# A hybrid recurrent, attention and mixture-of-experts block on one core: the expert weights in a ring of 23 buffers of 1 MB instead of 11 of 2 MB

## The chip, the cores and the metric

The kernel runs on one core of one Trainium2 chip. Time is the device time of one execution in microseconds (us), the median of several runs. Lower is better.

## The reference

One layer works on 256 frames of 1024 numbers, all in float32. A mixer comes first: an input projection, a gated linear recurrence, a forgetting attention with 16 heads, and three output projections. Then every expert's feed-forward net is applied to the frames that chose it (4 of 32 experts for each frame), and a last RMS norm closes the layer:

```python
logits = (t @ w_router) + b_router
top_v, top_i = lax.top_k(logits, TOP_K)
combine = sum(one_hot(top_i, 32) * softmax(top_v)[..., None], axis=1)
for e in range(32):
    gu = t @ w_gate_up[e] + b_gate_up[e]          # 1024 x 2048 weights
    gate = jnp.minimum(gu[:, :1024], 7.0)
    up = jnp.clip(gu[:, 1024:], -7.0, 7.0)
    glu = gate * sigmoid(1.702 * gate)
    y = ((up + 1.0) * glu) @ w_down[e] + b_down[e]  # 1024 x 1024 weights
    out = out + combine[:, e:e + 1] * y
return rmsnorm(x + out, g_final)
```

The weights of one expert are 12 MB (a MB in this text is 2^20 bytes where buffers are counted), those of all 32 are 384 MB. Every one is read once. The mixer's weights are 40 MB.

## The kernel before, in words

The program is written engine by engine, with semaphores by hand. Each of the five queues runs its instructions in the order of the code.

**The mixer** has 40 weight chunks of 1 MB (`MIX_CHUNKS`), loaded by SyncE (SP) into a ring of eight buffers (`mix`), each split into a high and a low part by ScalarE (`split`) and VectorE (`split_lower`), and used by TensorE in `chunk`. The chunks are ten groups of four; `C_WO` = 36 is the last, the output projection. After it come the router and the choice of the experts.

**The experts** are worked through in order, n = 0 to 31, in pairs p. An expert's weights are 12 chunks of 1 MB (8 of `w_gate_up`, 4 of `w_down`), loaded as six pieces of 2 MB (`load_piece`, lines 286 and 287) into a ring of 11 slots (`N_SLOTS`). The slots lie in memory that the mixer has used: `free_after` (lines 297 to 303) names for each slot the semaphore that tells when the mixer is done with it. From piece 11 on, a piece waits until TensorE has used up the piece that had its slot (`chunk_done`). Piece 0 is issued ahead of mixer chunk 36, the others after mixer chunk 39. Only the last piece of all is cut in two DMAs (lines 290 and 291).

Up to 64 frames are gathered for each expert (`gather_half`), so TensorE's matmuls have 64 rows, and two of them run side by side. For one expert TensorE runs `gate_up` (L1254, 8 chunks), waits for VectorE and ScalarE to make the activation (`glu_of`, `sigmoid_of`), transposes it (`transpose_act`, L1266), runs `down` (L1278, 4 chunks), and after ScalarE's copy `Y_copy` (L610) adds the result to four accumulators in PSUM (`scatter`, L1285). In this way the work of one expert's activation lies between its `gate_up` and its `down`; the scatter of the expert before fills part of that time.

**The end**: after the last scatter ScalarE squares and sums the accumulators, four of 512 columns (L649), VectorE adds the halves (L1027), ScalarE takes the root (L654), VectorE scales by it and by `g_final` (L1032), and SP stores two tiles of 128 frames (L344).

**GpSimd** issues three groups of DMAs: the recurrence's gate weights (L390), the experts' biases (L396, L399), and `g_final` (L411), the last when slot 6 is free for good.

## Time and profile before

| | |
|---|---|
| median of 3 runs | 1217.91 us (1216.41 to 1218.07) |
| profiled execution, own time | 1219.77 us |
| its span, first to last instruction | 1217.7 us |
| mean granted TensorE clock | 0.995 |
| TensorE matmul busy | 1164.5 us (96%) |
| DMA moved | 449.84 MB, of these 447.80 MB read from HBM |
| longest chain, by engine | PE 61%, DMA 35% |

The span is 2.07 us shorter than the profiled execution's own time, and that execution is 1.86 us longer than the median of the others. In the profile PE is TensorE's matmul and PEld its weight load. L1254 is a line of the kernel. A row's last bracket is the idle time ahead of it and what ended that. A DMA "packet" is one contiguous run that one of the core's 16 DMA engines moves. GB/s and MB in the profile are decimal.

### The profile page before, as it was taken

How to read it: one execution, taken by the hardware profiler on the slowest of the kernel's cores; microseconds unless marked ns; L12 is line 12 of the kernel's file. 1: busy time of each engine (PE TensorE's matmuls, PEld its weight loads, DVE VectorE, ACT ScalarE, POOL GpSimd, SP SyncE). 2: the span in 40 equal slices, each digit the busy share in tenths (PEclk: the TensorE clock that was granted, in tenths of full speed). 3: DMA queues.
4: the chain of work that ended last, by engine and by line, in shares of the span. 5: the costliest groups of instructions: out<-in, count | busy, mean ns of one | idle time of the engine just before them, and what ended most of it. 6: DMA issues, size and time to landing. Idle time of an engine off the chain costs nothing.

```text
span 1217.7 us, 14789 instructions
## 1 busy us (share of the span) xinstructions
PE 1164.5 (96%) x6482; PEld 609.6 (50%) x6482; DVE 339.5 (28%) x651; ACT 260.1 (21%) x432; POOL 22.7 (2%) x40
## 2 busy tenths in 40 slices
PE   8999999999999999999999999999999999999985
PEld 8998999998334333333343333333333333333321
DVE  5686976564111110101021110101010101010101
ACT  6557566444001000000011010000000000000002
POOL 3000000201000000000000000000000000000000
PEclk9999999999999999999999999999999999999998
DMA  9954445768999999999999999999999999999993
GB/s 247 343 165 132 147 147 203 238 260 364 427 428 428 427 425 429 428 428 427 427 428 427 427 427 428 427 428 427 428 428 428 426 427 428 428 428 427 428 426 132
DMA packets 73643, 449.84 MB, mean 369 GB/s; under 512 B 6877, under 2 KB 47913, under 8 KB 48873
## 3 DMA queue, kind: packets, MB, share of 16 engines
q1 hardware_dynamic: 72784, 446.99, 89.8%
q0 software_dynamic: 656, 1.84, 0.6%
q8 instruction: 53, 0.87, 0.3%
q14 instruction: 14, 0.11, 0.0%
q10 hardware_dynamic: 136, 0.04, 0.0%
HBM read 447.80 MB, written 1.05 MB: 369 GB/s over the span
## 4 chain that ended last, share of the span: by engine, by line
PE 61%; DMA 35%; ACT 2%; DVE 2%; issue 1%; ACTq 0%; DVEq 0%
DMA slot<-in_w_gate_up 34%; PE pj L1254 19%; PE pj L1082 16%; PE gb L1278 11%; PE gb L1241 3%; PE pt L1285 2%; PE s L1285 2%; PE pj L1266 1%; PE ga L1241 1%; PE gb L1271 1%; PE pj L1247 1%; PE s L1141 1%; DVE w_lo L692 1%; DMA rows<-in_conv_w 0%; ACT w_hi L453 0%
## 5 line engine op out<-in xcount | busy, mean ns | idle before, releaser
L1254 PE MATMUL pj<-slot,GL 128*64 128x512 f32 x2048 | 453.4, 595 | 31.2 <-DMA slot<-in_w_gate_up 31.2
L1254 PEld LDWEIGHTS pj<-slot,GL 128*64 128x64 f32 x2048 | 141.3, 137 | 326.8 <-issue 263.5
L1278 PE MATMUL gb<-slot,x_sb 128*64 128x512 f32 x1024 | 227.1, 596 | 0.0
L969 DVE TENSOR_SCALAR x_sb<-pj 128x512 f32<-128x512 f32 x32 | 22.1, 691 | 730.9 <-PE pj L1254 730.9
L1278 PEld LDWEIGHTS gb<-slot,x_sb 128*64 128x64 f32 x1024 | 70.7, 137 | 136.2 <-issue 136.2
L598 ACT ACTIVATE x_sb<-x_sb 128x512 f32<-128x512 f32 x32 | 20.2, 630 | 513.0 <-DVE x_sb L969 513.0
L1082 PE MATMUL pj<-hT_hi,w_hi 128*128 128x256 f32 x432 | 123.4, 286 | 0.0
L1082 PE MATMUL pj<-hT_hi,w_lo 128*128 128x256 f32 x432 | 122.0, 283 | 0.0
L1082 PE MATMUL pj<-hT_lo,w_hi 128*128 128x256 f32 x432 | 120.2, 278 | 0.0
L692 DVE TENSOR_TENSOR w_lo<-mix,w_hi 128x1024 fp32r<-128x1024 f32 x80 | 96.1, 1242 | 44.2 <-ACT w_hi L453 43.7
L453 ACT ACTIVATE w_hi<-mix 128x2048 fp32r<-128x2048 f32 x40 | 76.6, 1915 | 77.3 <-PE pj L1082 70.5
L1082 PEld LDWEIGHTS pj<-hT_lo,w_hi 128*128 128x128 f32 x432 | 81.9, 190 | 0.2
L1082 PEld LDWEIGHTS pj<-hT_hi,w_hi 128*128 128x128 f32 x432 | 81.2, 188 | 0.2
L1082 PEld LDWEIGHTS pj<-hT_hi,w_lo 128*128 128x128 f32 x432 | 81.0, 188 | 0.0
L610 ACT ACTIVATE Y<-gb 128x512 f32<-128x512 f32 x32 | 19.1, 597 | 238.2 <-PE gb L1278 238.2
L1285 PE MATMUL s<-Y,GL 64*128 64x512 f32 x128 | 36.1, 641 | 0.7 <-ACT Y L610 0.7
L1285 PE MATMUL po<-Y,GL 64*128 64x512 f32 x64 | 36.8, 655 | 0.0
L1285 PE MATMUL pt<-Y,GL 64*128 64x512 f32 x64 | 36.8, 655 | 0.0
L1241 PEld LDWEIGHTS ga<-GL,x 128*128 128x128 f32 x256 | 29.8, 191 | 12.4 <-issue 12.2
L1241 PEld LDWEIGHTS gb<-GL,x 128*128 128x128 f32 x256 | 29.8, 191 | 12.2 <-issue 12.2
L602 ACT ACTIVATE x_sb<-pj 128x512 f32<-128x512 f32 x32 | 19.1, 597 | 67.5 <-PE pj L1266 67.5
L1241 PE MATMUL ga<-GL,x 128*128 128x128 f32 x256 | 32.8, 281 | 0.0
(297 smaller groups left out, 985.5 us busy)
## 6 DMA issues: line engine op xcount, KB each, us to landing
slot<-in_w_gate_up SPq DMA_DIRECT2D x128, 2048.0 KB, 44.8
slot<-in_w_down SPq DMA_DIRECT2D x63, 2048.0 KB, 43.9
mix<-in_w_in SPq DMA_DIRECT2D x28, 1024.0 KB, 8.4
mix<-in_w_lru_out SPq DMA_DIRECT2D x4, 1024.0 KB, 5.4
mix<-in_w_fox_out SPq DMA_DIRECT2D x4, 1024.0 KB, 5.8
mix<-in_w_o SPq DMA_DIRECT2D x4, 1024.0 KB, 5.6
slot<-in_w_down SPq DMA_DIRECT2D x2, 1024.0 KB, 45.9
x_sb<-in_x SPq DMA_DIRECT2D x2, 512.0 KB, 4.4
```

The source lines that it names most:

```text
L453: act.activation(w_hi[c % 2][:, :, :], mix[c % MIX_RING].rearrange("p (k n) -> p k n", k=KT), ACT.Identity).then_inc(hi_ready, 1)
L598: act.activation(sig, gate, ACT.Sigmoid, scale=ALPHA).then_inc(sig_ready, 1)
L602: act.activation(actT, pj[0][:, :].rearrange("p (j h s) -> p j h s", h=2, s=SLOTS), ACT.Identity).then_inc(actT_ready, 1)
L610: act.activation(Y, gb[:, :], ACT.Identity).then_inc(y_ready, 1)
L692: v.tensor_tensor(w_lo[c % 2][:, half, :], src[:, half, :], w_hi[c % 2][:, half, :].bitcast(F32), ALU.subtract).then_inc(ready, 1)
L969: v.tensor_scalar(gate, pj[0][:, :], LIMIT, None, ALU.min).then_inc(gate_ready, 1)
L1082: last = mm(pj[b][:, a * S:(a + 1) * S], lhs, rhs, start=(k == 0 and n == 0), stop=(k == KT - 1 and n == 2))
L1141: mm(ps[h][:, c0:c0 + n], Q[r0:r0 + HD, j, q * P:(q + 1) * P], K[r0:r0 + HD, j, 0:n], start=True, stop=False)
L1241: last = mm((ga, gb)[b][:, k % 4 * P:(k % 4 + 1) * P], x2[:, t, k * P:(k + 1) * P], sel[:, t, :, :], start=(t == 0), stop=(t == TT - 1))
L1254: last = mm(pj[q // 2][h:h + SLOTS, :], hg[:, c, i, :], w[:, q * 512:(q + 1) * 512], start=False, stop=(c == GU_CHUNKS - 1))
L1278: last = mm(gb[h:h + SLOTS, :], actT[:, f % 4, f // 4, :], w[:, a * D + q * 512:a * D + (q + 1) * 512], start=False, stop=(f == KT - 1))
L1285: last = mm(acc[t][q][:, :], selWT[h:h + SLOTS, i, t * P:(t + 1) * P], Y[h:h + SLOTS, :], start=first, stop=True, skip_group_check=True)
```

## The change

1. The ring has 23 slots of 1 MB. Every chunk is a DMA of its own (`load_expert_chunk`): 384 in place of 192 + 1. A piece was one contiguous run of 16 KB for each of 128 partitions; a chunk is half of that run, 8 KB, and the next 8 KB are the next chunk. Two of the slots lie in memory that nothing used (`spare_at` and the new `spare2_at`; the room comes from `tri`, `ones`, `Y` and the smaller scratch of GpSimd's DMAs).
2. Chunks 0 to 3 are issued among the mixer's (`EARLY`: ahead of mixer chunks 20, 24, 32 and 36).
3. The DMAs of GpSimd are issued by SP: gate weights after mixer chunk 7, biases after expert chunk 4, `g_final` behind the last expert chunk.
4. The last two experts, 30 and 31, are loaded and worked together: gate-up of 30, gate-up of 31, down of 30, down of 31 (`ORDER`). Expert 30's activation has a place of its own, `actT_late`.
5. At the end each square runs over 1024 columns, two PSUM banks, in one instruction, and its root follows at once; VectorE's additions are gone; the output is stored in four DMAs of 128 x 512.

```diff
-N_SLOTS = 11
-SCRATCH = 4096
-SLOT_OF = [q % N_SLOTS for q in range(ALL_PIECES)]
+ORDER = [(e, c) for e in range(N_EXP - 2) for c in range(EXP_CHUNKS)]
+ORDER += [(e, c) for lo, hi in ((0, GU_CHUNKS), (GU_CHUNKS, EXP_CHUNKS)) for e in (N_EXP - 2, N_EXP - 1) for c in range(lo, hi)]
+PLACE = {ec: q for q, ec in enumerate(ORDER)}
+N_SLOTS = 23
+SCRATCH = 1024
+SLOT_OF = [q % N_SLOTS for q in range(ALL_CHUNKS)]
+EARLY = {20: 0, 24: 1, 32: 2, 36: 3}
...
+            def chunk_src(e, c):
+                return piece_src(e, c // 2)[:, c % 2 * CHUNK:(c % 2 + 1) * CHUNK]
...
-                    sp.wait_ge(chunk_done, MIX_CHUNKS + 2 * USER_BEFORE[q] + 2)
-                (load_piece if q + 1 < ALL_PIECES else load_last_piece)(q // EXP_PIECES, q % EXP_PIECES, s)
+                    sp.wait_ge(chunk_done, MIX_CHUNKS + USER_BEFORE[q] + 1)
+                sp.dma_start(slot[s][:, :], chunk_src(*ORDER[q])).then_inc(loaded[s], 16)
...
-                if c == C_WO:
-                    load_expert_piece(0)
+                if c in EARLY:
+                    load_expert_chunk(EARLY[c])
...
+            load_expert_chunk(len(EARLY))
+            for i in range(4):
+                sp.dma_start(bgu_raw[i * N_EXP:(i + 1) * N_EXP, :].rearrange("e (q n) -> e q n", q=2),
+                             b_gate_up.rearrange("e (q h n) -> h e q n", q=2, h=2)[i // 2]).then_inc(late_loaded, 16)
...
+            sp.wait_ge(chunk_done, MIX_CHUNKS + LAST_USER[END_SLOT] + 1)
+            sp.dma_start(gfin_b, g_final.rearrange("(a n) -> a n", a=1).broadcast_to([P, D])).then_inc(gfin_loaded, 16)
...
             for t in range(TT):
                 act.wait_ge(scattered, TT * N_EXP - 1 + t)
-                for h in range(2):
-                    act.activation(junk, acc[t][h][:, :], ACT.Square,
-                                   accum_out=stat[:, 40 + 2 * t + h:41 + 2 * t + h]).then_inc(sumsq3, 1)
-                    act.wait_ge(sumsq3, 2 * t + h + 1)
-            for t in range(TT):
-                act.wait_ge(sum3_ready, t + 1)
+                act.activation(junk[t], acc_pair[t][:, :], ACT.Square, accum_out=stat[:, 66 + t:67 + t]).then_inc(sumsq3, 1)
+                act.wait_ge(sumsq3, t + 1)
                 act.activation(stat[:, 64 + t:65 + t], stat[:, 66 + t:67 + t], ACT.Sqrt, scale=1.0 / D,
...
+            pe.wait_ge(actT_ready, N_EXP - 1)
+            pe.wait_ge(selwt_ready, PAIRS)
+            gate_up(1, lambda c: chunk_of(N_EXP - 1, c))
+            down(0, lambda c: chunk_of(N_EXP - 2, c), actT_late)
+            pe.wait_ge(act_ready, N_EXP)
+            transpose_act()
+            pe.wait_ge(y_ready, N_EXP - 1)
+            for t in range(TT):
+                scatter(0, t)
+            pe.wait_ge(actT_ready, N_EXP)
+            down(1, lambda c: chunk_of(N_EXP - 1, c))
```

**SP's queue around mixer chunk 36.** `mix_53` to `mix_56` are the mixer's chunks 36 to 39, `slot_83` on are the expert slots. Before:

```order
L287 DMA slot_83<-in_w_gate_up 128x4096 [waits ylru_ready,s_psum]
L327 DMA mix_53<-in_w_o 128x8x256 [waits lo_back_ready,lo_front_ready]
...
L327 DMA mix_56<-in_w_o 128x8x256 [waits lo_back_ready,lo_front_ready]
L287 DMA slot_84<-in_w_gate_up 128x4096 [waits o_lo_ready,o_hi_ready,o_psum]
L287 DMA slot_85<-in_w_gate_up 128x4096 [waits lo_back_ready,lo_front_ready]
```

And now:

```order
L316 DMA slot_86<-in_w_gate_up 128x2048 [waits s_psum]
L332 DMA mix_53<-in_w_o 128x8x256 [waits lo_back_ready,lo_front_ready]
...
L332 DMA mix_56<-in_w_o 128x8x256 [waits lo_back_ready,lo_front_ready]
L316 DMA slot_87<-in_w_gate_up 128x2048 [waits o_psum]
L343 DMA raw<-in_b_gate_up 32x2x512 x4
L346 DMA raw<-in_b_down 32x512 x4
L316 DMA slot_88<-in_w_gate_up 128x2048 [waits o_lo_ready,o_hi_ready]
```

Each slot's row has half the columns, three chunks stand further up (ahead of the rows shown), and the eight bias DMAs now stand between the fifth chunk and the sixth.

**TensorE's queue in expert 31, the last.** From its last gate-up slot to its down, before:

```order
L1254 MATMUL pj<-slot_85,GL 64x512 x7
L1285 MATMUL s<-Y,GL 128x512 [waits y_ready]
L1285 MATMUL s<-Y,GL 128x512
L1266 MATMUL pj<-ident,x_sb 128x128 [waits act_ready]
...
L1271 MATMUL gb<-bdn,onehot 128x512 [waits actT_ready]
L1278 MATMUL gb<-slot_86,x_sb 64x512 [waits slot3_loaded]
```

And now, from the same place:

```order
L1259 MATMUL pj<-slot_90,GL 64x512 x3
L1276 MATMUL gb<-bdn,onehot 128x512
L1283 MATMUL gb<-slot_91,actT_late 64x512 [waits slot8_loaded]
...
L1283 MATMUL gb<-slot_94,actT_late 64x512 x3
L1271 MATMUL pj<-ident,x_sb 128x128 [waits act_ready]
L1271 MATMUL pj<-ident,x_sb 128x128 x3
L1290 MATMUL s<-x_sb,GL 128x512 [waits y_ready]
...
L1276 MATMUL gb<-bdn,onehot 128x512 [waits actT_ready]
L1283 MATMUL gb<-slot_95,x_sb 64x512 [waits slot12_loaded]
```

Expert 30's down (`actT_late`) stands where TensorE waited for expert 31's activation, and both scatters of expert 30 stand between the two downs.

## Rows read from the trace of the kernel before

**Rows 1.** The page: what the DMA engines moved, in 40 slices of the span.

```profile
GB/s 247 343 165 132 147 147 203 238 260 364 427 428 428 427 425 429 428 428 427 427 428 427 427 427 428 427 428 427 428 428 428 426 427 428 428 428 427 428 426 132
```

**Rows 2.** Windows: PE, PEld, DVE, ACT, POOL busy, clock, DMA share, GB/s.

```profile
320.00:700.00 380.00, 379.94 (x1816) 146.26 (x1814) 58.04 (x126) 36.91 (x77) 0.00 (x0) 1.00 1.01 428
700.00:1140.00 440.00, 413.82 (x1945) 156.17 (x1943) 62.76 (x136) 39.77 (x84) 0.00 (x0) 1.00 1.01 428
```

**Rows 3.** Waits of PE from 250 us on: total, times, longest.

```profile
PE pj L1254 <- DMA slot<-in_w_gate_up: 31.2, 30, 2.5
```

**Rows 4.** Timeline of PE, the last gate-up piece of three experts: start, length.

```profile
1098.90 1.51 PE L1254 MATMUL pj<-slot,GL 128*64 128x512 f32 x6 [1.24 <-DMA slot<-in_w_gate_up]
1128.27 1.94 PE L1254 MATMUL pj<-slot,GL 128*64 128x512 f32 x8 [1.24 <-DMA slot<-in_w_gate_up]
1188.26 1.94 PE L1254 MATMUL pj<-slot,GL 128*64 128x512 f32 x8 [1.24 <-DMA slot<-in_w_gate_up]
```

**Rows 5.** The chain that ended last: mixer chunk 4, expert 0's gate-up.

```profile
41.66 5.69 PE pj L1082 x48
...
298.45 13.91 PE pj L1254 x64
```

**Rows 6.** Timeline of SP's issues: pieces 1, 9 and 11.

```profile
231.55 0.34 SPq L287 DMA_DIRECT2D slot<-in_w_gate_up  x1
286.12 0.33 SPq L287 DMA_DIRECT2D slot<-in_w_gate_up  x1
302.07 0.33 SPq L287 DMA_DIRECT2D slot<-in_w_down  x1
```

**Rows 7.** DMA view of 600 to 700 us.

```profile
DMA packets 2932, 42.72 MB, mean 427 GB/s; under 512 B 324, under 2 KB 324, under 8 KB 324
```

**Rows 8.** DMA view of 30 to 45 us, in 40 slices.

```profile
GB/s 210 276 341 330 341 347 350 350 347 350 350 350 347 344 350 352 347 347 371 341 333 360 350 352 350 347 350 350 350 350 347 350 350 350 347 344 350 350 350 358
DMA packets 5077, 5.15 MB, mean 343 GB/s; under 512 B 80, under 2 KB 5073, under 8 KB 5075
```

**Rows 9.** DMA view of 1188.4 to 1191.2 us.

```profile
DMA packets 118, 1.16 MB, mean 415 GB/s; under 512 B 12, under 2 KB 12, under 8 KB 12
q1 hardware_dynamic: 118, 1.16, 98.7%
```

**Rows 10.** DMA view of 1192.5 to 1197 us.

```profile
DMA packets 128, 0.96 MB, mean 213 GB/s; under 512 B 11, under 2 KB 11, under 8 KB 11
q1 hardware_dynamic: 128, 0.96, 51.3%
```

**Rows 11.** The page, DMA issues: KB each, us from issue to landing.

```profile
slot<-in_g_final POOLq DMA_DIRECT2D x1, 512.0 KB, 10.5
```

**Rows 12.** Timeline of the end, after expert 31's gate-up.

```profile
1191.84 1.13 PE L1285 MATMUL s<-Y,GL 64*128 64x512 f32 x4
...
1194.96 0.75 PE L1266 MATMUL pj<-ident,x_sb 128*128 128x128 f32 x4 [1.99 <-DVE x_sb L976]
...
1198.37 7.39 PE L1278 MATMUL gb<-slot,x_sb 128*64 128x512 f32 x32
...
1205.81 0.60 ACT L610 ACTIVATE Y<-gb 128x512 f32<-128x512 f32 x1 [9.46 <-PE gb L1278]
1207.83 0.58 ACT L649 ACTIVATE slot<-s 128x512 f32<-128x512 f32 x1
...
1210.69 0.29 ACT L654 ACTIVATE stat<-stat,epsc 128x1 f32<-128x1 f32 x1
...
1211.21 1.41 DVE L1032 SCALAR_TENSOR_TENSOR slot<-s,stat,slot 128x512 f32<-128x512 f32 x2
...
1213.92 0.74 DVE L1032 SCALAR_TENSOR_TENSOR slot<-po,stat,slot 128x512 f32<-128x512 f32 x1
```

**Rows 13.** Timeline of ScalarE: an instruction over 1024 columns.

```profile
280.97 1.14 ACT L571 ACTIVATE bgu_part<-raw,rest_row 128x1024 fp32r<-128x1024 f32 x1
```

**Rows 14.** Timeline of SP: the issue of the first half of the last piece.

```profile
1148.51 4.81 SPq L290 DMA_DIRECT2D slot<-in_w_down  x1
```

More of the change, by code:

```diff
@@ L100, in hybrid_block @@
         hl_at, xc_at = take(), take()
-        lp_at, _ = take(PADDED), take()
+        lp_at, spare_at = take(PADDED), take()
         hh_at, x_at = take(), take()
@@ L184, in hybrid_block @@
         gfin_b = slot[END_SLOT][:, 0:D]
-        junk = slot[END_SLOT][:, D:D + 512]
+        junk = [slot[END_SLOT][:, D:2 * D], yo[:, 1, :]]
         gate = flat(x_sb)[:, 0:512]
@@ L613, in _ @@
             hg_copy(0)
-            for n in range(N_EXP):
+            for n in range(N_EXP - 1):
                 sigmoid_of(n)
@@ L622, in _ @@
                     selWT_copy(n // 2)
-                if n == N_EXP - 1:
-                    act.wait_ge(flag_ready, 1)
-                    over = act.value_load(flag_i[0:1, 0:1], min_val=0, max_val=1)
-                Y_copy(n)
+                if n < N_EXP - 2:
+                    Y_copy(n)
+            sigmoid_of(N_EXP - 1)
+            act.wait_ge(chunk_done, MIX_CHUNKS + ALL_CHUNKS - DN_CHUNKS)
+            act.activation(Y, gb[:, :], ACT.Identity).then_inc(y_ready, 1)
+            actT_copy(N_EXP - 1)
+            act.wait_ge(flag_ready, 1)
+            over = act.value_load(flag_i[0:1, 0:1], min_val=0, max_val=1)
+            Y_copy(N_EXP - 1)
             with act.If(over > 0):
@@ L1268, in transpose_act, with down @@
                 last.then_inc(act_transposed, 1)
-            def down(i, chunk_at):
+            def down(i, chunk_at, actT=actT):
                 mm(gb[:, :], onehot[:, i, :], bdn[:, :], start=True, stop=False)
@@ L1292, in _, with chunk_of @@
             pe.wait_ge(bgu_split, 1)
-            for n in range(N_EXP):
+            def chunk_of(n, c):
+                q = PLACE[n, c]
+                pe.wait_ge(loaded[SLOT_OF[q]], 16 * USES[q])
+                return slot[SLOT_OF[q]][:, :]
+            for n in range(N_EXP - 1):
                 p, i = divmod(n, 2)
                 def chunk_at(c):
-                    q = n * EXP_PIECES + c // 2
-                    if c % 2 == 0:
-                        pe.wait_ge(loaded[SLOT_OF[q]], 16 * USES[q])
-                    elif q == ALL_PIECES - 1:
-                        pe.wait_ge(end_loaded, 16)
-                    return slot[SLOT_OF[q]][:, c % 2 * CHUNK:(c % 2 + 1) * CHUNK]
+                    return chunk_of(n, c)
                 if i == 0:
@@ L1331, in _ @@
                     scatter(1 - i, 1, n == 1)
+                if n == N_EXP - 2:
+                    break
                 pe.wait_ge(actT_ready, n + 1)
```

118 lines of the change are left out of this document (56 added, 62 removed).

## The prediction

> **What bounds the kernel now.** I read the DMA rate over the span first. From the eleventh slice (about 300 us) to the last but one it stands at 425 to 429 GB/s and doesn't move [rows 1]; before that the mixer's chunks ask for less. The windows give the same rate, 428 GB/s, in two stretches in which TensorE behaves differently: from 320 to 700 us it is busy for 379.94 of 380 us, from 700 to 1140 for 413.82 of 440 [rows 2]. So TensorE is the quicker of the two. It starts with a full ring at 298.45 us [rows 5], works it off, and from about 700 us on takes each piece as it lands: 31.2 us of waiting in 30 waits [rows 3]. The same piece of two neighbouring experts comes at 1098.90 and 1128.27 us, 29.37 us apart, or 4.90 us for a piece of 2 MB and 2.45 us for each MB [rows 4]. The reader should see that the kernel's length is a sum of three: when the ring's refill starts, the number of MB still to come times 2.45 us, and what TensorE does after the data. A faster TensorE gives nothing; a tenth of a microsecond a MB gives 36 us.
>
> The pieces of that sum: piece 11, the first that needs a slot which TensorE has used, is issued at 302.07 us [rows 6], 3.6 us after 298.45, since it waits for two chunks. The last gate-up piece lands at 1188.26 [rows 4]. Two pieces of down follow, so the last data lands about 1188.26 + 2 x 4.90 = 1198.1. `Y_copy` of the last expert starts at 1205.81 [rows 12], 7.7 us later: there TensorE waited for the activation, not for data, and down ran from 1198.37 without a stop. From 1205.81 to the span's end at 1217.7 are 11.9 us.
>
> **The change, part by part.** All against the profiled execution (span 1217.7).
>
> *More prefetch.* Before, 22 MB were in the ring when TensorE started; pieces 9 and 10 were issued from 286.12 us on [rows 6]. Now it is 23 MB. Can they all be there? Up to 286 us the new queue has 19 chunks whose releasers (the splits of mixer chunks 32 to 39, the attention, the merge) come no later than before; four of them, 4 MB, are ahead of 231.55 us, where before 2 MB were. The last four chunks are released at 286.12 and take 4 x 2.5 = 10 us, so they land about 298 us. The ring is full as before and holds 1 MB more: -2.45 us. Loading chunks 0 to 3 earlier gives nothing beyond that, since the ring's size, not its filling, sets what is left to load.
>
> *Finer release.* Chunk 23 waits for one chunk of expert 0 and not for two. Eight chunks take 13.91 us [rows 5], one 1.74: refill starts 1.75 us earlier. -1.75 us. Later on, finer slots are worth nothing: SP has long issued what the engines move, about ten pieces ahead of them.
>
> *8 KB packets.* This is the dear part. 361 chunks follow the refill's start, and each has eight packets of 8 KB for every DMA engine where there were four of 16 KB. Does a packet cost something of its own? For 16 KB: 427 GB/s over 16 engines [rows 7] is 26.7 bytes a ns for one, 614 ns a packet. For the mixer's 1 KB: the level slices stand at 350 [rows 8], 21.9 bytes a ns, 46.8 ns a packet, where 26.7 bytes a ns would make it 38.4. A straight line through the two (46.8 ns at 1 KB, 614 ns at 16 KB) has some 9 ns for the packet itself. Four more packets a MB: 35 ns, 1.4% of 2.45 us. 361 x 0.035 = +12.7 us. The trace also has 8 KB packets, of the piece that was already cut in two. From 1192.5 to 1197 us half the engines are busy (51.3%) and move 213 GB/s [rows 10]; twice that is 426, or 0.3% under 427: +2.7 us, the lower bound. From 1188.4 to 1191.2 nearly all are busy with them and move 415 at 98.7% [rows 9], 420 at a full share, 1.6% under 427 (+14 us); taken raw it is 2.9% (+25 us), the upper bound. I take the line's 12.7: the stretch with all engines busy is the one like the new steady state, and it is near.
>
> The Trainium skill, "DMA: Bandwidth & Descriptors", section "Why small descriptors are slow (HBM only)", puts a fixed overhead of about 3 cycles beside one cycle for each 32 bytes of a packet. By that, two packets of 8 KB cost 518 cycles against 515, 0.6%, and an estimate from it is +5.2 us in place of 12.7, which would bring the total to 1210. The rows with all engines busy speak for more than that; no row here shows one engine's cycles.
>
> *`g_final`.* Its 0.5 MB are issued by GpSimd at a time when every engine is full (10.5 us to land [rows 11]), so 0.52 MB / 427 GB/s = 1.2 us of them stand ahead of the last weights. Now they come behind the last chunk, and ScalarE's first square, which waits for them, comes later still. -1.2 us. If they landed late they would hold up the squares; the margin is about 3 us.
>
> *Gate weights and biases on SP.* The same bytes at nearly the same time. The gate weights go behind mixer chunk 7 and must be there when TensorE is done with chunk 4 of the mixer at 41.66 + 5.69 = 47.35 us [rows 5]; the ten MB up to and with them are through at about 37 us at the rate of the first two slices [rows 1]. The biases (0.75 MB) fill a gap behind 231.55 us and are used at 280.97 [rows 13]. 0 us. Without that cover they would cost what they are late.
>
> The last data then lands at 1198.1 - 2.45 - 1.75 + 12.7 - 1.2 = 1205.4 us.
>
> *Last two experts together.* Expert 30's down now stands where TensorE waited for expert 31's activation, and the last data are four chunks of down. Counted from the last landing L: the fourth chunk of expert 30's down lands at L - 9.9 and is worked through by L - 8.2. Then come the transposes (0.75), two scatters (1.13 each), the bias matmul (0.5) and four chunks of down (7.39 in [rows 12]; 7.0 is four times 1.75), together some 11 us with the handing over. `Y_copy` starts at L + 2.7: TensorE, not the last chunk (L + 1.9), decides by a little. That is 1208.1 against 1205.81: +2.3 us. Of the 7.7 us between data and copy 5.0 are gained, and the packets take more than that back.
>
> *The end.* Before, four squares stand between 1207.83 and 1210.69 [rows 12], then the root, then VectorE's scaling from 1211.21, done at 1213.92 + 0.74. A square over 1024 columns should take what ScalarE took for as many, 1.14 us [rows 13], with its readout 1.3, and the root of tile 0 starts at 1209.1 instead of 1210.69. Tile 1's square ends while VectorE scales tile 0, so its scaling begins when VectorE is free: about 2.0 us earlier in all. The last store is 256 KB and not 512: 0.6 us less. -2.6 us.
>
> **Sum**: +2.3 - 2.6 = -0.3 us. The median is 1217.91, so 1217.6.
>
> **Rivals.** (1) *Packets are nearly free*: what half the engines do alone [rows 10] holds with all 16. Then 2.7 stands for 12.7 and the time is 1207.6; halfway, 1212.6. For it: it is a direct reading of the right packet size from the right tensor. Against it: [rows 9], and the 1 KB line [rows 8]. The skill's rule named above lies between it and my value. 25%, halfway cases counted.
> (2) *Packets cost more*, slower: contention between 16 full engines is paid by packet, as the 415 of [rows 9] read raw: +25 us, 1230; at 1.6 to 2% it is 1219 to 1223. It decides from 1.4 + 0.7 = 2.1% for a loss of 6 us, and from 1.7% for one of 0.2%. 22%.
> (3) *The end goes wrong*: TensorE now waits 0.7 us ahead of each of the last chunks. The mean granted clock was 0.995 and the last down took 7.39 us and not 7.0, so a little of that was there at the end before. If the granted clock fell to its lower level, 1.2 GHz, for half of the last down and the scatters, their 9 us would grow by 2 to 4 us: 1220. 8%.
> (4) *The finer queue doesn't work*: the issue of one of the last DMAs took 4.81 us [rows 14] where others take 0.33 [rows 6], so SP's queue seems to take only about ten at a time. With 1 MB each that is 10 MB, 25 us of work; the engines don't run dry. It would matter below one or two DMAs. 2%.
> The forecast has the rest, 43%, its own range 1214.5 to 1221.
>
> **How the numbers follow.** One nanosecond a packet is 1.4 to 2.9 us of time (four more packets a MB, or all eight), which is why the range is wide: from halfway into rival 1 (1210) to a packet cost of 2.2% (1224). A measurement of this kernel can tell about 0.2%, 2.4 us, from no change. Faster by more than that: rival 1 and the forecast's lower quarter, 36%. Within: 37%. Slower: rival 2, part of 3, the forecast's upper end, 27%.
>
> **What would show it.** Experts that TensorE takes in step with the data should be 29.8 us apart and not 29.37; the steady rate should fall from 427 to about 421 GB/s; if SP's queue takes ten DMAs, the time from issue to landing should be some 25 us for a chunk. The refill should start at 300.3, `Y_copy` of expert 31 at about 1208, the last scaling should end some 6.9 us after it and not 8.9. A rate still at 427 makes rival 1 right; 415 or less makes rival 2 right. If mixer or router end later than before (TensorE's first expert matmul not at 298.45), something moved to SP's queue was in the way, and the whole sum shifts.

## The result, and the profile after

| | before | after |
|---|---|---|
| median | 1217.80 us (20 runs, 1216.26 to 1219.56) | 1219.57 us (20 runs, 1218.74 to 1222.24) |
| ratio to before, 95% interval | | 1.0015 (1.0009 to 1.0022) |
| profiled execution, own time | 1219.77 us | 1218.76 us |
| its span | 1217.7 us | 1217.0 us |
| mean granted TensorE clock | 0.995 | 0.997 |

The changed kernel is 1.8 us slower; the forecast was 0.3 us faster. The two profiled executions say the opposite of the medians: the span of the changed kernel is 0.7 us shorter. The explanation has to account for both.

The page of the changed kernel, GB/s moved in 40 slices of the span, beside [rows 1]:

```profile
GB/s 286 325 181 153 176 185 178 211 302 324 421 421 421 421 421 421 421 421 422 421 421 421 421 421 421 421 421 421 421 421 421 421 421 421 421 421 421 421 421 253
```

The level part has gone from 425 to 429 down to 421. The windows of the same kernel, with the columns of [rows 2], say that TensorE is as busy as before and so still the quicker of the two:

```profile
320.00:700.00 380.00, 379.95 (x1816) 146.32 (x1814) 58.05 (x126) 36.91 (x77) 0.00 (x0) 1.00 1.01 421
700.00:1140.00 440.00, 412.73 (x1914) 150.76 (x1910) 60.17 (x130) 39.17 (x83) 0.00 (x0) 1.00 1.01 421
```

Its waits from 250 us on (total, times, longest) are as long together as in [rows 3] and nearly twice as many, one for each MB in place of each two:

```profile
PE pj L1259 <- DMA slot<-in_w_gate_up: 28.7, 53, 1.4
```

The timeline of TensorE, changed kernel: two last gate-up chunks that lie two experts apart, and then the last three waits for data of all (start, length, idle time ahead in brackets):

```profile
1075.97 1.94 PE L1259 MATMUL pj<-slot,GL 128*64 128x512 f32 x8 [0.53 <-DMA slot<-in_w_gate_up]
...
1135.61 1.94 PE L1259 MATMUL pj<-slot,GL 128*64 128x512 f32 x8 [0.54 <-DMA slot<-in_w_gate_up]
...
1190.28 1.94 PE L1283 MATMUL gb<-slot,actT_late 128*64 128x512 f32 x8 [0.34 <-DMA slot<-in_w_down]
1192.76 1.94 PE L1283 MATMUL gb<-slot,actT_late 128*64 128x512 f32 x8 [0.54 <-DMA slot<-in_w_down]
1195.24 1.94 PE L1283 MATMUL gb<-slot,actT_late 128*64 128x512 f32 x8 [0.55 <-DMA slot<-in_w_down]
1197.11 0.75 PE L1271 MATMUL pj<-ident,x_sb 128*128 128x128 f32 x4
...
1200.22 7.09 PE L1283 MATMUL gb<-slot,x_sb 128*64 128x512 f32 x32
```

59.64 us for two experts is 29.82 for one, where [rows 4] had 29.37. The last wait is for the fourth chunk of expert 30's down. Expert 31's down follows from 1200.22 without a stop, so TensorE's queue and not the last landing (1204.64, by the count further down) sets the last copy. The rest of the end, beside [rows 12]:

```profile
1207.36 0.60 ACT L617 ACTIVATE x_sb<-gb 128x512 f32<-128x512 f32 x1 [8.87 <-PE gb L1283]
...
1209.37 1.00 ACT L660 ACTIVATE slot<-s 128x1024 f32<-128x1024 f32 x1
...
1210.50 0.30 ACT L662 ACTIVATE stat<-stat,epsc 128x1 f32<-128x1 f32 x1
...
1211.10 1.41 DVE L1037 SCALAR_TENSOR_TENSOR slot<-s,stat,slot 128x512 f32<-128x512 f32 x2
...
1212.61 1.41 DVE L1037 SCALAR_TENSOR_TENSOR slot<-pt,stat,slot 128x512 f32<-128x512 f32 x2
```

From the copy to the span's end are 9.64 us where there were 11.9.

For the ledger further down I added up, in the traces, the packets of 8 KB and more, and took the time from the span's start at which the n-th MB had been moved (384 MB of weights and 1 MB of the program's own instructions). The last column is the landing of the last weights. This is a count of mine over the packets, not a view of the profile; the kernels other than before and after are the experiments below.

```
kernel                       24 MB   30 MB   40 MB  100 MB  200 MB  360 MB  380 MB     last
before                       308.3   323.0   347.4   494.6   739.8  1132.2  1182.5  1197.60
e1_before_again              306.6   321.2   345.6   492.8   738.0  1130.5  1180.8  1195.81
e12_sp_dmas_only             306.5   321.2   345.6   492.8   738.0  1130.4  1179.4  1194.47
e6_one_dma_8kb               306.5   321.3   346.2   495.6   744.6  1143.0  1194.1  1209.46
e3_halves_by_column          308.2   323.0   347.8   497.3   746.3  1144.7  1195.8  1211.22
e7_ring_of_22                304.7   319.7   344.6   494.1   743.1  1141.5  1191.3  1206.78
after                        301.9   317.4   342.3   491.8   740.8  1139.3  1189.0  1204.64
e2_after_again               302.1   317.4   342.4   491.8   740.8  1139.4  1189.2  1204.88
e10_old_order_at_end         302.1   317.4   342.3   491.8   740.8  1139.3  1189.1  1204.60
e4_pieces_new_end            307.7   322.3   346.7   493.9   739.2  1131.6  1180.6  1195.83
e8_pieces_fine_start         304.7   319.9   346.0   493.0   738.3  1130.8  1179.8  1195.84
e11_pieces_one_more_mb       303.8   319.8   345.4   492.5   737.8  1130.2  1179.2  1195.08
```

In before, e3 and e4 TensorE's first expert matmul came 1.8, 1.9 and 1.1 us later than in e1, and their marks lie later by about as much.

### The profile page after: what moved, and what is told of

Its sections match the earlier page's. It is cut to its first block, busy times and chain, and to the rows that moved or that the text cites. A ratio compares the mean times of both kernels' runs of the same rounds, so it can differ in the third digit from the quotient of the medians.

```text
span 1217.0 us, 14979 instructions
## 1 busy us (share of the span) xinstructions
PE 1168.3 (96%) x6482; PEld 605.2 (50%) x6482; DVE 338.9 (28%) x649; ACT 259.5 (21%) x428; POOL 15.1 (1%) x27
## 4 chain that ended last, share of the span: by engine, by line
PE 54%; DMA 41%; ACT 2%; DVE 2%; SPq 1%; issue 1%; DVEq 0%; ACTq 0%
DMA slot<-in_w_gate_up 38%; PE pj L1259 18%; PE pj L1087 16%; PE gb L1283 9%; DMA slot<-in_w_down 2%; PE gb L1246 1%; PE s L1290 1%; PE pt L1290 1%; PE ga L1246 1%; PE pj L1271 1%; PE pj L1252 1%; DMA mix<-in_w_in 1%; PE s L1146 1%; DVE w_lo L700 1%; ACT w_hi L460 1%
## 5 line engine op out<-in xcount | busy, mean ns | idle before, releaser
L1259 PE MATMUL pj<-slot,GL 128*64 128x512 f32 x2048 | 459.5, 597 | 29.3 <-DMA slot<-in_w_gate_up 28.7
L1259 PEld LDWEIGHTS pj<-slot,GL 128*64 128x64 f32 x2048 | 138.8, 136 | 333.6 <-issue 244.7
L1283 PE MATMUL gb<-slot,x_sb 128*64 128x512 f32 x992 | 219.7, 595 | 0.0
L617 ACT ACTIVATE x_sb<-gb 128x512 f32<-128x512 f32 x31 | 18.5, 597 | 230.7 <-PE gb L1283 230.7
L1290 PE MATMUL s<-x_sb,GL 64*128 64x512 f32 x128 | 36.1, 641 | 0.7 <-ACT x_sb L617 0.7
L1290 PE MATMUL pt<-x_sb,GL 64*128 64x512 f32 x128 | 35.9, 638 | 0.0
L1246 PE MATMUL gb<-GL,x 128*128 128x128 f32 x256 | 32.7, 281 | 0.0
## 6 DMA issues: line engine op xcount, KB each, us to landing
slot<-in_w_gate_up SPq DMA_DIRECT2D x256, 1024.0 KB, 26.9
slot<-in_w_down SPq DMA_DIRECT2D x128, 1024.0 KB, 26.9
```

The costliest lines, as they stand in the source:

```text
L617: act.activation(Y, gb[:, :], ACT.Identity).then_inc(y_ready, 1)
L1246: last = mm((ga, gb)[b][:, k % 4 * P:(k % 4 + 1) * P], x2[:, t, k * P:(k + 1) * P], sel[:, t, :, :], start=(t == 0), stop=(t == TT - 1))
L1259: last = mm(pj[q // 2][h:h + SLOTS, :], hg[:, c, i, :], w[:, q * 512:(q + 1) * 512], start=False, stop=(c == GU_CHUNKS - 1))
L1283: last = mm(gb[h:h + SLOTS, :], actT[:, f % 4, f // 4, :], w[:, a * D + q * 512:a * D + (q + 1) * 512], start=False, stop=(f == KT - 1))
L1290: last = mm(acc[t][q][:, :], selWT[h:h + SLOTS, i, t * P:(t + 1) * P], Y[h:h + SLOTS, :], start=first, stop=True, skip_group_check=True)
```

## The experiments

The kernel before was run again beside each group; its medians there were 1217.99 (e1 to e4), 1217.74 (e5 to e8), 1217.78 (e9 to e11) and 1218.09 us (e12). The leading theory was that 8 KB packets cost what the change gains elsewhere. A second theory (A in the expectations) was that one of the two profiled executions wasn't typical.

**e1: the kernel before again.** No edit.

> The kernel before, unchanged. The two profiled executions differ by 0.7 us of span (217.7 and 217.0 past 1000 us) but the medians by 1.8 us the other way. Theory A: the profiled execution of before happened to start badly: TensorE's clock stood at its lower level at about 15 to 19 us, under the first mixer chunk's matmuls, and that cost it about 1.9 us; another profile of the same kernel starts its mixer stretch at about 19.4 us and not 21.1, starts expert 0's gate-up at about 296.6 and ends at a span of about 1215.8. Rival B: before always starts like that (expert 0's gate-up again at 298.4, span 1217.7), and the profiled execution of after was a lucky one. Time against before: ratio 1.000 (within 0.1%).

Measured: 1217.91 us (1216.38 to 1219.86, 11 runs), ratio 0.9996 (0.9987 to 1.0005). Its profiled execution took 1217.95 us, the median, with a span of 1216.0. The windows from 14 to 18 us, first of before, then of e1 (columns as in [rows 2], the clock is the last but two):

```profile
14.00:18.00 4.00, 3.78 (x20) 3.65 (x19) 4.00 (x9) 2.11 (x2) 0.00 (x0) 0.57 1.16 309
```

```profile
14.00:18.00 4.00, 3.78 (x32) 3.75 (x32) 4.00 (x10) 2.00 (x2) 0.00 (x0) 1.00 1.16 308
```

And the timelines of TensorE in the first mixer chunk, before and then e1:

```profile
14.76 1.91 PE L1099 MATMUL gb<-hT_hi,w_hi 128*128 128x256 f32 x8
16.47 1.80 PE L1099 MATMUL pj<-hT_hi,w_lo 128*128 128x256 f32 x8
18.11 1.11 PE L1099 MATMUL gb<-hT_hi,w_lo 128*128 128x256 f32 x8
```

```profile
14.59 1.12 PE L1099 MATMUL gb<-hT_hi,w_hi 128*128 128x256 f32 x8
15.55 1.12 PE L1099 MATMUL pj<-hT_hi,w_lo 128*128 128x256 f32 x8
16.51 1.12 PE L1099 MATMUL gb<-hT_hi,w_lo 128*128 128x256 f32 x8
```

Same kernel, same instructions, but in the first profile eight products take 1.91 us at the lower level of the clock (1.2 GHz) and in the second 1.12 at 2.4 GHz. In e1 the stretch of lower clock lay earlier, from 9.6 to 13.0 us, mostly under transposes; the mixer's products that follow wait for ScalarE anyway, and those of 14.59 start no later than in before. What follows keeps the distance: expert 0's gate-up and the last gate-up piece in e1 stand at

```profile
296.63 3.65 PE L1254 MATMUL pj<-slot,GL 128*64 128x512 f32 x16
...
1186.48 3.65 PE L1254 MATMUL pj<-slot,GL 128*64 128x512 f32 x16 [1.24 <-DMA slot<-in_w_gate_up]
```

where [rows 5] and [rows 4] had 298.45 and 1188.26. Theory A holds: the profile on which the prediction was built lost 1.8 us at its start and is that far above its median. It is compared with e1 from here on. (The places of such stretches in the expectations of e1, e8 and e9 were counted from a point about 0.7 to 1.7 us ahead of the span's start; the times in this text count from the span's start, as the profile does.)

**e2: the changed kernel again.** No edit.

> The changed kernel, unchanged. Theory A: its profile again has expert 0's gate-up at about 296.6 us and a span of 1217 to 1218; ratio to before 1.0015. Rival B: its start differs from run to run, and this profile starts expert 0 later, at about 298.4, with a span of about 1219.

Measured: 1219.93 us (1218.64 to 1221.4, 11 runs), ratio 1.0012 (1.0003 to 1.0021), span 1218.1. Expert 0 starts at 296.66 and all data of e2 lie within 0.3 us of after's in the table. Theory A as expected: the undisturbed starts of both kernels are the same, so the change moved nothing there. Of the 1.1 us by which e2's span is longer than after's, 0.25 lie ahead of the last copy and 0.83 behind the last scaling: from the end of VectorE's last scaling to the end of the span are 3.02 us in after and 3.85 in e2, with the same instructions. e2's own time, 1219.93, is its kernel's median; after's, 1218.76, is among its fastest.

**e3: every piece in two DMAs, left and right half.** In the kernel before:

```diff
-                sp.dma_start(slot[s][:, :], piece_src(e, m)).then_inc(loaded[s], 16)
+                sp.dma_start(slot[s][:, 0:CHUNK], piece_src(e, m)[:, 0:CHUNK]).then_inc(loaded[s], 16)
+                sp.dma_start(slot[s][:, CHUNK:], piece_src(e, m)[:, CHUNK:]).then_inc(loaded[s], 16)
```

> The kernel before, but every 2 MB piece is loaded by two DMAs of 1 MB, the left and the right half of each partition's 16 KB, so in packets of 8 KB; slots, releases and the end are as before. Packet theory: the steady rate falls from 427 to 421 GB/s as in the changed kernel, 361 MB after the refill's start cost some 35 ns more each, +12.5 us (1230.5, ratio 1.0103). Rival, the rate falls for another reason (the finer ring, the order of slots): the rate stays 427 GB/s and the time within 3 us of before.

Measured: 1232.06 us (1231.26 to 1233.2), ratio 1.0106 (1.0091 to 1.0122), +14.1 us. The page of e3:

```profile
GB/s 246 343 157 137 154 154 200 247 267 361 423 421 422 420 421 422 421 422 422 421 420 422 421 422 421 421 422 421 421 421 421 421 421 422 422 421 421 421 420 135
```

421, as in the changed kernel, with the ring, the releases and the end of before. The rate falls with the DMAs alone. Its profiled start was disturbed as before's was, and against that profile the span is 13.7 us longer.

**e6: as many DMAs as before, packets of 8 KB.** In the kernel before, one DMA of 2 MB takes the left (or right) halves of two neighbouring pieces; TensorE uses the chunks in that order:

```diff
-                sp.dma_start(slot[s][:, :], piece_src(e, m)).then_inc(loaded[s], 16)
+                sp.dma_start(slot[s][:, :].rearrange("p (a n) -> p a n", a=2), split_src(e, m)).then_inc(loaded[s], 16)
```

> The kernel before with its 2 MB DMAs, as many as before, but each takes 8 KB per partition from two places: the left (or the right) halves of two neighbouring pieces, so a DMA has 256 packets of 8 KB. TensorE takes the chunks in the stored order (0, 2, 1, 3, ...). Packet theory: rate 421 GB/s and a time near e3's 1232. Rival, the number of DMAs costs: 427 GB/s and 1218.

Measured: 1229.50 us (1229.08 to 1231.51), ratio 1.0097 (1.0082 to 1.0112), +11.8 us; the profiled execution is the slowest of the four. The page of e6:

```profile
GB/s 262 345 148 130 170 139 205 259 266 362 423 421 421 421 421 422 421 421 421 421 420 421 421 421 421 422 421 421 421 421 420 421 421 421 421 421 421 421 421 134
```

and its last gate-up piece on TensorE's timeline:

```profile
1200.06 3.65 PE L1263 MATMUL pj<-slot,GL 128*64 128x512 f32 x16 [1.31 <-DMA slot<-in_w_gate_up]
```

This run separates the packet from the DMA. From the 24th to the 360th MB e1 takes 823.9 us, e6 836.5, e3 836.5: half as many DMAs as e3 and the same time. The cost is the packet's: 12.6 us over 336 MB, 37.5 ns a MB. (e3's median is 2.6 us above e6's, four runs each; by the marks none of that comes from the steady stretch.) The last gate-up piece is 13.58 us later than e1's.

**e5: two DMAs, partitions 0 to 63 and 64 to 127.** Packets stay at 16 KB:

```diff
-                sp.dma_start(slot[s][:, :], piece_src(e, m)).then_inc(loaded[s], 16)
+                sp.dma_start(slot[s][0:64, :], piece_src(e, m)[0:64, :]).then_inc(loaded[s], 16)
+                sp.dma_start(slot[s][64:P, :], piece_src(e, m)[64:P, :]).then_inc(loaded[s], 16)
```

> The kernel before, every 2 MB piece loaded by two DMAs of 1 MB as in e3, but cut the other way: partitions 0 to 63 and 64 to 127, so the packets stay at 16 KB. It has as many DMAs, issues and completions as e3. Packet theory: the size of the packet is what costs, so the rate is 427 GB/s and the time is that of before (1217.9, within 2 us). Rival, each DMA has a cost of its own (its start, its completion, SP's issue): the rate is near 421 and the time near e3's 1232.

Measured: 1685.8 us (six runs that scatter from 1526.9 to 1983.2). Neither theory: a miss, and useless for the count of DMAs, which e6 settled. The page of e5, from an execution of 1556.6 us with a mean granted clock of 0.940:

```profile
GB/s 283 255 135 163 137 231 219 220 228 223 222 224 223 225 227 241 268 280 306 320 327 341 347 363 373 372 375 378 354 367 370 362 347 373 373 367 371 367 306 114
```

Once expert pieces flow, the rate is about 220, half of before's, and creeps up to 370, never to 427. In the stretch from 600 to 700 us the engines count as fully busy and move 267 GB/s. A DMA that fills half the partitions is a different transfer from one that fills all; the traces don't show what it is held up by, and that stays open.

**e7: a ring of 22.** The changed kernel with one slot less:

```diff
-N_SLOTS = 23
+N_SLOTS = 22
...
-        slot_at = [spare_at, spare2_at, lg_at, k_at, v_at, q_at, *mix_at[0:5], hl_at, lp_at, mix_at[5], mix_at[6], xc_at, mix_at[7],
+        slot_at = [spare_at, lg_at, k_at, v_at, q_at, *mix_at[0:5], hl_at, lp_at, mix_at[5], mix_at[6], xc_at, mix_at[7],
...
-        END_SLOT = ALL_CHUNKS % N_SLOTS
+        END_SLOT = EXP_CHUNKS
```

> The changed kernel without the buffer that the change made room for: 22 slots of 1 MB, 22 MB of prefetch as before. If the length is the sum that the prediction made (refill's start plus the MB still to come at the rate), one more MB comes after the refill's start: 2.5 us more than the changed kernel, about 1222.3. Rival, the 23rd slot is not filled in time or the end isn't bound by data: the same time as the changed kernel, 1219.8.

Measured: 1221.47 us (1221.31 to 1223.54), ratio 1.0039 (1.0026 to 1.0052), 1.5 to 1.9 us over the changed kernel (its two medians). The data come as expected: at the 24th MB e7 is 2.8 us behind after, from the 30th to the 380th 2.3, and the last landing is 2.1 us later (1.9 against e2). The medians show a little less, and the spans 2.6 (after) and 1.5 (e2), since the time behind the last scaling is another in each: 3.46 us in e7, 3.02 in after, 3.85 in e2. Half a microsecond is lost right at the refill's start: after took 40.4 us for the 16 MB from the 24th to the 40th, e7 39.9 and e6 39.7.

**e4: the old ring with the new end.** The changed kernel with 11 slots of 2 MB in the places that they had before, only piece 0 loaded early, the last four pieces cut in two:

```diff
-N_SLOTS = 23
+N_SLOTS = 11
...
-                    sp.wait_ge(chunk_done, MIX_CHUNKS + USER_BEFORE[q] + 1)
-                sp.dma_start(slot[s][:, :], chunk_src(*ORDER[q])).then_inc(loaded[s], 16)
+                    sp.wait_ge(chunk_done, MIX_CHUNKS + 2 * USER_BEFORE[q] + 2)
+                e, c = ORDER[2 * q]
+                if q < ALL_PIECES - CUT:
+                    sp.dma_start(slot[s][:, :], piece_src(e, c // 2)).then_inc(loaded[s], 16)
```

> The changed kernel with the ring of before: 11 slots of 2 MB, packets of 16 KB, 22 MB of prefetch; only the last four pieces are cut in two. The last two experts together, the end and SP's DMAs are as in the changed kernel. Packet theory: the rate is 427 GB/s again and the last data lands at the time of before less 1.2 us for the final gain's bytes; the new end gives 5.0 us between last data and last copy and 2.3 us behind the copy: 8.5 us under before, 1209.3. Rival, the end's gain is not worth that in a full run because TensorE waits for data ahead of its last chunks at a lower clock: 1213 or more.

Measured: 1210.75 us (1209.13 to 1211.01), ratio 0.9928 (0.9914 to 0.9941), 7.2 us under before. The packet theory's side, 1.5 us short of its number. Its profile lost 1.1 us in the router (expert 0 starts at 297.71): the window from 289 to 293 us has a clock of 0.68, with TensorE's small products and stay-awake products in it.

```profile
289.00:293.00 4.00, 4.00 (x27) 4.00 (x27) 1.68 (x11) 2.02 (x4) 0.00 (x0) 0.68 1.03 442
```

**e8: e4 with a finer start of the refill.**

```diff
+                elif q == N_SLOTS:
+                    e, c = ORDER[2 * q]
+                    for h in range(2):
+                        sp.wait_ge(chunk_done, MIX_CHUNKS + h + 1)
+                        sp.dma_start(slot[s][:, h * CHUNK:(h + 1) * CHUNK],
+                                     piece_src(e, c // 2)[:, h * CHUNK:(h + 1) * CHUNK]).then_inc(loaded[s], 16)
```

> As e4, but piece 11, the first that needs a used slot, is cut in two DMAs of 1 MB, the first issued when TensorE is done with one chunk and not with two. If the data sets the time, all that follows comes 1.8 us earlier: 1209.0 against e4's 1210.75. e4's own profile lost 1.1 us in the router, where TensorE's clock stood at the lower level from 289.1 to 292.5 us; a profile without that has expert 0's gate-up at 296.6. Rival, TensorE itself is the bound at the end (in e4 it waited for data last at about 1157 us): it is data-bound until then, so the gain is passed on there too; only if the gain is nothing would the refill's start not matter.

Measured: 1210.35 us (1209.26 to 1212.39), ratio 0.9941 (0.9928 to 0.9954), the same as e4. The refill did start earlier: the 24th MB is there at 304.7 us against 307.7, of which 1.4 us are e4's late start (expert 0 at 296.30 in e8, 297.71 in e4). Against e12, which has the same ring and starts at 296.60, the head start is 1.8 us at the 24th MB (304.7 and 306.5); at the 40th e8 is 0.4 us behind (346.0 and 345.6). All of it was gone. The DMA views of 318 to 324 us, e8 and then e4:

```profile
DMA packets 134, 1.93 MB, mean 322 GB/s; under 512 B 16, under 2 KB 16, under 8 KB 16
```

```profile
DMA packets 180, 2.56 MB, mean 426 GB/s; under 512 B 24, under 2 KB 24, under 8 KB 24
```

In e8 the engines run short there: TensorE is between expert 0's gate-up and its down, uses up no chunk, and so frees no slot, while the refill has no queue behind it yet. SP's next issue is at 318.88, when two chunks of down are done (down starts at 315.18). In e4 the same pause is covered because its refill starts later. The changed kernel has the early start and doesn't run short, since its slots come free after one chunk: SP issues at 317.37, and the same view shows 415 GB/s, near the level 421:

```profile
DMA packets 344, 2.49 MB, mean 415 GB/s; under 512 B 41, under 2 KB 41, under 8 KB 41
```

My expectation had missed this.

**e9: more warm-up.** The kernel before with `for _ in range(20)` in place of 14 at the first products.

> The kernel before with 20 in place of 14 warm-up products on TensorE ahead of its first transposes, so that TensorE is busy up to the landing of the first rows at about 8.5 us. In seven profiles so far a stretch at the lower clock, about 3.4 us long, lay at 10.4 to 16.1 us (six of them) or was absent there (one); when it lay under the first mixer chunk (before, e3) the mixer started 1.7 us late. Clock theory: the stretch is set off by TensorE's idling near the start, so without the idle gap it is earlier or missing and the median falls from 1217.9 to about 1216.4, the fastest of before's runs. Rival, its place is chance and the gap doesn't matter: the median stays at 1217.9 (within 0.3).

Measured: 1217.82 us (1216.11 to 1219.7, 11 runs), ratio 0.9997 (0.9988 to 1.0006). The rival: TensorE was busy up to the rows, its profile had the stretch of lower clock at 14.2 to 17.6 us all the same, and the runs spread as before's do. (The expectation miscounts. Of the nine profiles up to then, e5's left out, six had the stretch near the start and three, e4, e7 and e8, had none.) What sets its place isn't settled.

**e10: experts 30 and 31 one after the other.** The changed kernel with

```diff
-ORDER = [(e, c) for e in range(N_EXP - 2) for c in range(EXP_CHUNKS)]
-ORDER += [(e, c) for lo, hi in ((0, GU_CHUNKS), (GU_CHUNKS, EXP_CHUNKS)) for e in (N_EXP - 2, N_EXP - 1) for c in range(lo, hi)]
+ORDER = [(e, c) for e in range(N_EXP) for c in range(EXP_CHUNKS)]
```

and the loops of before over the experts.

> The changed kernel, but experts 30 and 31 one after the other as in the kernel before (the ring, the squares, the stores and SP's DMAs stay). The prediction said that the pairing takes the stretch from the last landing to the last Y_copy from 7.7 to 2.7 us: 5.0 us more without it, 1224.9, and the stretch of lower clock that stands under the last down in before, e1, e3 and e6 comes back. Rival, what the pairing moves is lost elsewhere (TensorE's 31 us of waits give it back): less than 2 us more.

Measured: 1221.72 us (1221.66 to 1224.32), ratio 1.0039 (1.0025 to 1.0052), 1.8 to 2.2 us over the changed kernel (its two medians). A miss: 5.0 was expected, and the stretch of lower clock under the last down, which was to come back, didn't. The timeline of e10, TensorE and the last copy:

```profile
1195.17 1.94 PE L1253 MATMUL pj<-slot,GL 128*64 128x512 f32 x8 [0.55 <-DMA slot<-in_w_gate_up]
1197.04 1.13 PE L1284 MATMUL s<-x_sb,GL 64*128 64x512 f32 x4
1200.16 0.74 PE L1265 MATMUL pj<-ident,x_sb 128*128 128x128 f32 x4 [1.99 <-DVE x_sb L978]
...
1202.33 7.09 PE L1277 MATMUL gb<-slot,x_sb 128*64 128x512 f32 x32
...
1209.47 0.60 ACT L616 ACTIVATE x_sb<-gb 128x512 f32<-128x512 f32 x1 [7.92 <-PE gb L1277]
```

Only 14.3 us lie between the last gate-up data and the copy. In [rows 4] and [rows 12] they were 17.55 (1188.26 to 1205.81), in e1 17.6. Of the 3.3 us, some 1.7 is one chunk of gate-up: with pieces of 2 MB TensorE has two chunks to do after the last gate-up landing, with 1 MB one. The other 1.6 is the clock: up to the copy it is granted in full in e10, in before and e1 it isn't (e12 below has the old pieces and the full clock, and takes 16.0 us).

**e12: only the DMAs from GpSimd to SP.** In the kernel before:

```diff
-            g.wait_ge(chunk_done, MIX_CHUNKS + 2 * LAST_USER[END_SLOT] + 2)
-            g.dma_start(gfin_b, g_final.rearrange("(a n) -> a n", a=1).broadcast_to([P, D])).then_inc(gfin_loaded, 16)
...
+            sp.wait_ge(chunk_done, MIX_CHUNKS + 2 * LAST_USER[END_SLOT] + 2)
+            sp.dma_start(gfin_b, g_final.rearrange("(a n) -> a n", a=1).broadcast_to([P, D])).then_inc(gfin_loaded, 16)
```

and the gate weights and biases likewise.

> The kernel before, with that part of the change alone that moves GpSimd's DMAs to SP: gate weights behind mixer chunk 7, biases behind piece 1, the final gain behind the last piece. The prediction put 0 us on the first two and 1.2 us of gain on the last. If so, expert 0's gate-up starts at 296.6 us in an undisturbed start (as in e1), the last gate-up pieces of experts 29 and 31 come 58.75 us apart and not 60.0, and the time is 1216.6, ratio 0.999. Rival, something in SP's queue delays the ring's filling: expert 0's first wait or its refill comes later, and the time is that of before or more.

Measured: 1216.11 us (1215.09 to 1217.73, 11 runs), ratio 0.9982 (0.9973 to 0.9991), 2.0 us under before. The direction of the first theory, with more than its number. The windows over the stretch from the last gate-up work to the last copy, e1 and then e12:

```profile
1189.00:1205.00 16.00, 13.31 (x53) 4.25 (x51) 2.67 (x4) 2.13 (x4) 0.00 (x0) 0.89 0.22 90
```

```profile
1188.00:1202.00 14.00, 11.31 (x51) 3.76 (x49) 2.67 (x4) 2.06 (x4) 0.00 (x0) 1.00 0.32 131
```

and e12's last gate-up piece and last copy:

```profile
1185.15 3.65 PE L1254 MATMUL pj<-slot,GL 128*64 128x512 f32 x16 [1.24 <-DMA slot<-in_w_gate_up]
...
1201.15 0.60 ACT L610 ACTIVATE Y<-gb 128x512 f32<-128x512 f32 x1 [7.92 <-PE gb L1278]
```

The final gain's bytes are no longer ahead of the last weights: 1185.15 against 1186.48, 1.3 us. And from there to the copy are 16.0 us, not 17.6: in e1 TensorE waited for expert 31's gate-up three times, in e12 twice, and in this profile its clock didn't fall. Up to the 360th MB the data of e12 and e1 are within 0.1 us of each other: the gate weights and biases on SP's queue cost nothing. Behind the last scaling e12 takes 0.36 us more (3.41 and 3.05).

This profile is of one of e12's fast executions (1215.21; five of the eleven runs lie between 1215.1 and 1215.4, the other six between 1216.1 and 1217.7), and its span is 2.6 us under e1's. By the medians the gain is 2.0, so beyond the 1.3 of transfer a typical run gains 0.7 us, not 1.6, and whether the lower clock is away in every run isn't shown.

**e11: e4 with 23 MB prefetched.** The room of the 23rd buffer holds the first half of piece 11, once:

```diff
+                elif q == N_SLOTS:
+                    e, c = ORDER[2 * q]
+                    sp.dma_start(extra[:, :], piece_src(e, c // 2)[:, 0:CHUNK]).then_inc(extra_loaded, 16)
+                    sp.wait_ge(chunk_done, MIX_CHUNKS + 2)
+                    sp.dma_start(slot[s][:, CHUNK:], piece_src(e, c // 2)[:, CHUNK:]).then_inc(loaded[s], 16)
```

> As e4 (pieces of 2 MB, new end), with the room of the 23rd buffer used once: the first half of piece 11 goes there ahead of any release, so 23 MB are prefetched and one MB less comes after the refill's start. By e7 a MB of prefetch is worth 1.7 us and by the rate 2.45: 1208.4 to 1209.0 against e4's 1210.75. Rival, the end is TensorE's now (in e8 the data came 0.6 us earlier than in e4 and the end not at all): 1210.

Measured: 1209.53 us (1209.02 to 1210.2), ratio 0.9930 (0.9916 to 0.9943), between the two expectations, and the lowest median here: 8.3 us under before, 10 under the changed kernel. Its ratio and e4's (0.9928, 0.9914 to 0.9941) don't tell the two apart. As in e8, nearly all of the head start is gone by the 40th MB: against e12 it is 2.7 us at the 24th (303.8 and 306.5) and 0.2 at the 40th (345.4 and 345.6).

## Why the prediction was wrong

It was wrong on the sign, by 2.1 us, inside its range. Its steps, with e1 as the kernel before (e2's value behind after's where they differ):

| term | predicted | measured | from |
|---|---|---|---|
| 8 KB packets | +12.7 | +13.65 | last landing, e6 less e1 |
| finer release | -1.75 | -1.34 | last landing, e7 less e1, e12's and e6's shares taken off |
| ring, one MB more | -2.45 | -2.14 (-1.90) | last landing, after less e7 |
| gate weights, biases on SP | 0 | 0.0 | e12 less e1, 100 MB |
| `g_final` behind the weights | -1.2 | -1.34 | last landing, e12 less e1 |
| **last data** | **+7.3** | **+8.83 (+9.07)** | last landing, after less e1 |
| last data to last copy | -5.0 | -5.54 (-5.53) | 2.72 (2.73) after 8.26 us |
| copy to the end of the last scaling | -2.0 | -2.19 | 6.66 after 8.85 us |
| **last scaling to the span's end** | **-0.6** | **-0.03 (+0.80)** | 3.02 (3.85) after 3.05 us |
| **sum** | **-0.3** | **+1.1 (+2.1)** | spans; medians +1.8 |

That the five terms add to the last data's figure is no test of them: the finer release is the only one that wasn't taken from two kernels that differ in it alone, and its row is what is left. It has the earlier loading of chunks 0 to 3 in it as well.

*What bounds the kernel, and the sum of three.* Right. The level rate and the data's mark carried every experiment.

*8 KB packets.* Right in mechanism (e6 against e3) and nearly in size: 37.5 ns a MB over the level stretch where 35 was forecast, 421 GB/s as forecast. To the last landing it is 13.65 us, 1.0 more than forecast. Rival 1, packets nearly free, falls, and its witness had been misread: in [rows 10] the engines move 213 GB/s at a share of 51.3%, which is 415 at a full share, as [rows 9] had been reckoned, and not the 426 of doubling it. Of rival 2, only the direction was right; 1.5%, not 2.1. The Trainium skill's figure ("DMA: Bandwidth & Descriptors", "Why small descriptors are slow (HBM only)"), by which +5.2 us was estimated, isn't borne out here: measured is two and a half times that.

*More prefetch and finer release.* Predicted -4.2 together, measured -3.5 (-3.2), and the refill began as forecast (chunk 23 is issued at 298.49, 2.0 us after TensorE's start where piece 11 came 3.6 after it). Two sentences of the prediction don't hold in general. That only the ring's size and the refill's start set what follows is true only while the engines never run short again; with pieces of 2 MB they do around 320 us, and e8 lost its whole head start and e11 nearly all. That finer slots are worth nothing later on is wrong for the same place: they carry the changed kernel over the pause (415 GB/s where e8 has 322).

*Gate weights and biases.* Right: nothing, by the data (e12 and e1 within 0.1 us up to the 360th MB) and by TensorE's start of expert 0 (296.60 and 296.63).

*The last two experts.* The copy came 2.7 us after the last landing, as forecast, and at 1207.36 where 1208.1 was forecast. But I took the 5.0 us for the pairing's. The pairing is worth about 2 us: 1.8 to 2.2 by the medians of e10 and the changed kernel, 2.1 from last landing to copy (4.9 and 2.7). The rest of the term were things that it contained without naming: one chunk in place of two after the last gate-up landing (some 1.7), and the lower clock that stands under the last down in before and e1 (1.6).

*The end.* -2.6 forecast, -2.2 in after and -1.4 in e2. The root of tile 0 starts 3.14 us after the copy, 1.7 earlier than in [rows 12] (4.88), with a square of 1.00 us where 1.14 was assumed, and the scaling is done 2.2 us earlier, so that part was right. The 0.6 us for the smaller last store are not there: from the last scaling to the span's end before, e1, e3, e6 and e9 take 3.04 to 3.05 us, the seven profiles of kernels with four stores (after, e2, e4, e7, e8, e10, e11) 3.02 to 4.12, in the mean 3.7. e12, with two stores and SP's DMAs, takes 3.41; what makes the time longer there wasn't separated.

*Rivals 3 and 4.* The new end didn't lower the clock in any profile; the old end did in all five, and the change took that away. Issue to landing is 26.9 us, near the 25 by which SP's queue was read as ten DMAs, and harmless. The ten aren't general: e6's DMAs of 2 MB take 32.9 us, fewer than seven of them at 4.98 us each.

*Which step failed.* Two terms, both mis-sized in the direction of a gain. "Last data": 7.3 for 8.8 to 9.1, of that 1.0 for the packets, 0.4 for the release and 0.3 to 0.55 for the ring. And the smaller last store: -0.6 for 0.0 to +0.8. Together they are 2.1 to 3.2 us; the stretch from last data to copy gave back 0.5 and the scaling 0.2. With 1.8 us between the kernels, that is the sign. Beside it, the profile of before was atypical at its start by 1.8 us, and that of after was one of its kernel's fastest. That made the traces agree with my forecast to 0.8 us (span 1217.4 expected, 1217.0 found; last data 1205.4 expected, 1204.6 found) while the medians didn't: the agreement was luck, errors of the sum against an atypical baseline.

## What to carry to other kernels

Where a stream of large DMAs sets the time, keep the packets as large as the source allows and buy finer grain only at the two ends: the change's new end, SP's DMAs and its extra MB gave 1209.5 us with 16 KB packets and 1219.6 with 8 KB. A head start in a ring is worth its bytes only if the consumer frees slots steadily right after it; look for the first pause, and make the slots fine enough to cover it. And when the profiled execution lies a microsecond or two off its own median, find where before making a sum of terms that small: one more profile of the same kernel did it here, for the kernel before (e1) and for the changed one (e2).

## What the runs showed of the hardware that I had not expected

- The granted clock shows single short stretches at its lower level (1.2 GHz) whose place differs between executions of one kernel. In nine of thirteen profiles (e5's left out) one lies near the start, in before, e3 and e9 between 14.2 and 18.7 us, under the first mixer chunk, in the six others between 8.9 and 13.5. The late place costs 1.3 to 1.9 us (start of expert 0 in e9, before and e3 against e1), the early one nothing that shows. In e4 one lay in the router, 288.1 to 291.6 us, and cost 1.1. Six profiles (e1, e3, e4, e6, e8, e9) have one between 979 and 1014 us, where TensorE has slack; e1's last gate-up piece shows no price for it.
- Under the last down before, e1, e3, e6 and e9 have one, 5 of 5 profiles with unchanged end and `g_final` on GpSimd, and neither e12 nor any kernel with the new ring or the new end has it (after, e2, e4, e7, e8, e10, e11). It cost 1.6 us (e1 against e12). It isn't there in every run of the kernel before: of its 62 runs beside e1 to e12, five with a granted clock of 0.998 leave no room for it (the stretch behind the last matmul, 5 us or more in every profile, takes the missing 0.002), and they are among the fastest, 1216.2 to 1216.4 us against 1217.4 to 1218.4 for most. That moving one 0.5 MB DMA behind the weights takes it away rests on e12's one profile.
- 8 KB packets cost 1.5% against 16 KB with all 16 engines busy, whether in 193 DMAs (e6) or in 384 (e3).
- DMAs into 64 partitions at a time, with the same 16 KB packets, ran at 220 to 375 GB/s where 128 partitions ran at 427 (e5).
- The time from the last scaling to the span's end is the same to 0.01 us in five profiles of the old end (3.04 to 3.05), and 3.02 to 3.85 in two profiles of the changed kernel.
